# A hybrid DeltaNet and attention trunk: lower-half transfers issued one round later, scores and maxima three blocks ahead

## What is computed

```python
proj = h @ w_in + b_in                     # 16 query heads, 4 key and 4 value heads of width 64
q, k = apply_rope(q), apply_rope(k); v = ...
# chunks of 64 tokens; every chunk sees itself and the chunk before it
scores = einsum(q, k_band) * 64 ** -0.5
m = maximum(max(scores), sink)
pexp = exp(scores - m)
probs = pexp / (sum(pexp) + exp(sink - m))
o = einsum(probs, v_band)
h = h + (o @ w_out + b_out)
```

## Time and profile before

| | |
|---|---|
| median of 3 runs | 1548.16 us (1547.15 to 1553.75) |
| profiled execution | 1545.53 us, span 1543.6 us |
| mean granted TensorE clock | 0.971 of full speed |
| TensorE matmuls busy | 95% of the span |
| VectorE, ScalarE, GpSimd busy | 52%, 35%, 17% |
| keys, queries and values projected, from the first matmul to the first scores | 904.6 to 1004.6 us |
| 16 blocks, to the first output matmul | 1004.6 to 1077.0 us |

### The profile page before, as it was taken

The page is one execution under the profiler, slowest core; times in us unless marked ns, Lnnn a source line. Parts: engine busy times, 40 slices in busy tenths (PEclk is TensorE's granted clock), DMA queues, the critical chain, the costliest instruction groups (busy, mean ns, idle before and its releaser), DMA issues.

```text
span 1543.6 us, 19377 instructions
## 1 busy us (share of the span) xinstructions
PE 1467.2 (95%) x7270; PEld 1210.0 (78%) x7270; DVE 801.0 (52%) x1132; ACT 541.4 (35%) x820; POOL 262.6 (17%) x268
## 2 busy tenths in 40 slices
PE   6799999999988999999999986798999999999998
PEld 4688888888876888888888864666888888888877
DVE  4546666566657434343456664547443343434755
ACT  6333434434214314232234431145342322323444
POOL 3534435444303100000002110000201000000111
PEclk9799999999999999999999998959999999999999
DMA  5221221210112232323222326320323232323221
GB/s 144 55 55 28 55 55 27 54 37 31 41 55 95 84 109 82 109 82 108 94 98 82 94 44 140 85 60 16 109 96 109 82 110 82 109 82 109 83 82 55
DMA packets 163810, 120.73 MB, mean 78 GB/s; under 512 B 44417, under 2 KB 161442, under 8 KB 163746
## 3 DMA queue, kind: packets, MB, share of 16 engines
q1 hardware_dynamic: 152210, 116.71, 25.2%
q10 hardware_dynamic: 11536, 3.15, 0.9%
HBM read 112.50 MB, written 2.10 MB: 74 GB/s over the span
## 4 chain that ended last, share of the span: by engine, by line
PE 76%; DVE 10%; ACT 5%; issue 3%; ACTq 2%; DVEq 2%; POOL 1%; DMA 0%; POOLq 0%
PE psum L148 21%; PE psum L150 21%; PE psum L149 21%; PE psum L825 3%; PE psum L816 3%; DVE wL L140 2%; ACT wH L132 2%; PE psum L832 1%; ACTq L1693 1%; DVE bL L1269 1%; ACT taps L671 1%; DVE hT L1457 1%; PE psum L1800 1%; ACTq L1698 1%; DVE acc L1455 1%
## 5 line engine op out<-in xcount | busy, mean ns | idle before, releaser
L148 PE MATMUL psum<-aH,wH 128*128 128x512 f32 x896 | 364.2, 407 | 7.8 <-DVE wL L140 4.3
L150 PE MATMUL psum<-aL,wH 128*128 128x512 f32 x896 | 351.3, 392 | 0.0
L149 PE MATMUL psum<-aH,wL 128*128 128x512 f32 x896 | 351.1, 392 | 0.0
L140 DVE TENSOR_TENSOR wL<-wRaw,wH 128x2048 fp32r<-128x2048 f32 (+2 forms) x126 | 250.6, 1992 | 159.9 <-ACT wH L132 154.2
L148 PE MATMUL psum<-bH,wH 128*128 128x512 f32 x720 | 288.4, 401 | 25.9 <-DVE pleT L1878 19.9
L150 PE MATMUL psum<-bL,wH 128*128 128x512 f32 x720 | 283.4, 394 | 0.0
L149 PE MATMUL psum<-bH,wL 128*128 128x512 f32 x720 | 283.4, 394 | 0.0
L132 ACT CAST wH<-wRaw 128x2048 fp32r<-128x2048 f32 (+2 forms) x110 | 199.2, 1815 | 220.5 <-PE psum L150 191.8
L148 PEld LDWEIGHTS psum<-aH,wH 128*128 128x128 f32 x896 | 169.8, 189 | 41.2 <-DVE wL L140 4.7
L150 PEld LDWEIGHTS psum<-aL,wH 128*128 128x128 f32 x896 | 169.2, 189 | 36.2
L149 PEld LDWEIGHTS psum<-aH,wL 128*128 128x128 f32 x896 | 169.8, 190 | 30.7 <-issue 0.5
(11 more groups left out here) (289 smaller groups left out, 1725.8 us busy)
## 6 DMA issues: line engine op xcount, KB each, us to landing
wRaw<-in_mlp_w_up SPq DMA_DIRECT2D x64, 512.0 KB
wRaw<-in_mlp_w_down SPq DMA_DIRECT2D x64, 512.0 KB
wRaw<-in_dn_w_in SPq DMA_DIRECT2D x32, 512.0 KB
wRaw<-in_ple_w_gate SPq DMA_DIRECT2D x16, 512.0 KB
wRaw<-in_sw_w_in SPq DMA_DIRECT2D x16, 256.0 KB
wRaw<-in_sw_w_out SPq DMA_DIRECT2D x16, 256.0 KB
wRaw<-in_dn_w_out SPq DMA_DIRECT2D x8, 384.0 KB
work<-in_x SPq DMA_DIRECT2D x4, 512.0 KB, 5.1
```

The source lines that it names most:

```text
L140: last = [nc.vector.tensor_tensor(o, r, h_.bitcast(F32), ALU.subtract) for o, r, h_ in zip(*([v if half is None else v[:, half * v.shape[1 ...
L148: nc.tensor.matmul(o, wh, xh, start=first, stop=False)
L149: nc.tensor.matmul(o, wl, xh, start=False, stop=False)
L150: return nc.tensor.matmul(o, wh, xl, start=False, stop=last)
```

## The change

Two edits. In the projection, ScalarE issues the lower-half transfers of round j-1 in round j, after `prep_hi` of panel j+1 and before the copies of round j; those of the last round are issued after the loop, as before. In the blocks, scores and maxima run three blocks ahead instead of two, and `mxs` gets a third slot.

```diff
-        mxs = sqSum[:, 0:12 * GRP].rearrange("p (s a j) -> p s a j", s=2, a=6)
+        mxs = sqSum[:, 0:18 * GRP].rearrange("p (s a j) -> p s a j", s=3, a=6)
...
             scores(0)
             scores(1)
+            scores(2)
             for i in range(ATB):
-                if i + 2 < ATB:
-                    scores(i + 2)
+                if i + 3 < ATB:
+                    scores(i + 3)
...
                 prep_hi(act, n0 + j + 1, (n0 + j + 1) % 2)
                 if j == 0:
                     norm_act(act, u - 1)
+                if j:
+                    for f in range(2):
+                        stack(act, j - 1, f, 1)
                 for f in range(2):
                     act.wait_ge(qk_r, 2 * j + f + 1)
                     if j >= 4:
                         act.wait_ge(k_hi_moved[f], 16 * KVH * 2)
                     nc.scalar.copy(qkHi[j % 4][:, f, :], rot[2 * f]).then_inc(qk_hi, 1)
-                for f in range(2):
-                    stack(act, j, f, 1)
+            for f in range(2):
+                stack(act, GRP, f, 1)
...
-                t, mx = i // KVH, mxs[:, i % 2]
+                t, mx = i // KVH, mxs[:, i % 3]
...
-                t, g, mx = i // KVH, i % KVH, mxs[:, i % 2]
+                t, g, mx = i // KVH, i % KVH, mxs[:, i % 3]
...
             maxima(0)
             maxima(1)
+            maxima(2)
             for i in range(ATB):
-                mx = mxs[:, i % 2]
+                mx = mxs[:, i % 3]
...
-                if i + 2 < ATB:
+                if i + 3 < ATB:
                     dve.drain()
-                    maxima(i + 2)
+                    maxima(i + 3)
```

## The result

The changed kernel took 1531.35 us in the median of 4 runs (1527.39 to 1540.26), the kernel before 1548.76 us in 4: ratio 0.989, 95% interval 0.9841 to 0.9939. It is faster, as forecast, but by 17.4 us where 23.5 were forecast, and 1531.35 lies 0.85 us above the end of the range: the prediction was wrong. The profiled execution took 1527.39 us, span 1525.5 us, 18.1 us less than the one before.

The account below looks back on a forecast made before the run. In the projection TensorE waited on a ring through ScalarE's DMA issues. From a median of 1548.2 us, moving the transfers took off 23.5 and three ahead 0, giving 1524.7, rounded 1524.5 us; range 1511 to 1530.5.

Parts of the forecast that it names:

- the ring through ScalarE's issues: Projection: ScalarE's DMA issues delay the next cast, making rounds of 16.5 us where TensorE needs 11.2; moving them saves 23.5.
- round 2: Projection: the keys' 16 issues on ScalarE make the copies 2.8 us late, leaving TensorE one 2.8 us wait before round 3.
- a load that I had put at 6: Projection: a panel load takes 6 us; panel 3's, issued at 929.27, is due at 938.75, 9.5 us later.
- panel 4: Projection: its load lands at 945.0, 4.4 us before it is due; stretched by sharing engines, at 948, still in time.
- the clock after that wait: Projection, after the 2.8 us wait: a slower TensorE clock costs 0 or 1.6 us; 0.4 was taken.
- edit 2 cuts no link of the ring: Blocks: with scores and maxima both three ahead the order is unchanged, so two blocks at full clock still take 6.8 us.
- two blocks under 6.5 us: Blocks: sign that the prediction is wrong, meaning the ring has a link less.
- I take 0: Blocks: running three ahead gains zero, between bounds of 6.7 us won and 3.4 us lost.
- The sum: Whole kernel: 1545.5 - 23.5 = 1522.0 us for an execution like the profiled one; 1524.7 for the median, rounded 1524.5.
- a case with half clock in all blocks: Rival: the clock stays low through all blocks, ten more costing 22.6 us; 1547 us, no change; chance 0.04.
- full clock in the blocks: Rival: after the shorter wait the early blocks keep full clock, 11.3 us less, 1513 us; chance 0.22.

Follow-up runs that it names:

- edit 1 alone: Against the kernel before, only the lower-half transfers are issued one round later, scores and maxima staying two ahead; 1525.57 us, ratio 0.9854.
- edit 2 alone: Against the kernel before, only scores and maxima run three blocks ahead, transfers as before; 1551.79 us, ratio 1.0023.
- the first experiments: First follow-up kernels, sharing one chip session, edit 1 alone and edit 2 alone among them; the kernel before took 1547.38 us in 17 runs.
- The second set of the changed kernel: The changed kernel run again unaltered, against the kernel before on the same chip; median 1524.77 us of 6, ratio 0.9845.

## Why the prediction was right and where it was wrong

**Right: the ring through ScalarE's issues.** The casts follow the copies, TensorE's wait of 10.5 us is gone, those before round 4 and before the values too. From round 0's copies to the first scores it was 81.4 us before, 58.3 after; the forecast was 57.4. The change's gain up to there was shown by undoing: edit 1 alone gives the whole difference (58.3 us), edit 2 alone almost none of it (81.2).

**Right in size, half right in cause: round 2.** I let ScalarE's 16 issues begin when the cast had ended. They begin 0.25 us after it has started, beside it, and the copies came 12.25 us after round 0's in one profile and 13.41 in the other, instead of 14.2. In the second they were late by the issues, as forecast, though by about 1 us; in the first they were in time, and the landing of panel 3 stood in their place: issued at 928.41, first used at 937.18, 8.8 us for a load that I had put at 6. TensorE's wait was 2.1 us either way, not 2.8. The Trainium skill's rule in "DMA: Bandwidth & Descriptors", section "Issuing engines are not separate DMA queues", that all issuing engines share the same DMA engines, agrees with the 8.8 us: the load ran beside transfers of both queues. I weighed it for panel 4, which the cast waited 0.28 us for, and not for panel 3.

**Mis-sized, small: the clock after that wait.** I took 0.4 us between 0 and 1.6. It fell in both profiles of the changed kernel, 12.7 us for the round at 0.87, so the term was 1.6 there. Of the eleven profiles with edit 1 it fell in six, after waits of 1.81 and 2.05 to 2.14 us, and not in five, after 1.74 to 1.86. From the copies to the scores the six took 57.9 to 58.3 us, the five 56.3 to 56.5; the 57.4 of the forecast had no clock term in it. So the term is not a size between two bounds but one of two cases, and the 58.3 came near 57.4 because a wait shorter than forecast made up for part of the clock.

**Right: edit 2 cuts no link of the ring.** Two blocks took 6.77 us. That the order and not the distance closes the ring was then shown by the kernel with the maxima two ahead, 6.20 us. The prediction's sign of a ring with a link less, "two blocks under 6.5 us", is what that kernel shows.

**Wrong: "I take 0" for the blocks, and with it the top of the range.** This is the step that failed. The sum, "for an execution like the profiled one", carried over the half-clock stretch of one profile, 38 us, as if it belonged to the kernel, and gave its length no term. Measured, the stretch was 52.1 us in the profiled execution and the blocks took 5.5 us more. Its length differs between executions of one program, 41.6 and 52.1 us, and was 89.7 us for edit 1 alone. At 0.38 us for each, that is 1.3, 5.3 and 19.6 us more. I had a case with half clock in all blocks, at 22.6 us, but gave it 0.04. The kernel before has it too: 3 of its 17 runs beside the first experiments took 1564.65 to 1567.2 us, at a mean clock of 0.954, where most took 1545 to 1549 at 0.966 to 0.971. Its three runs that I had, 1547.15 to 1553.75 us, already differed by 6.6 us, and the range should have taken that in. The second set of the changed kernel, 1524.77 us, is the forecast; the first, 1531.35, is outside the range. The sum came out for executions with a short stretch, and the range had no term for the others. That the second set met the forecast within 0.3 us is luck too: it needed five short executions out of six. The opposite case, full clock in the blocks, was priced too high: of the five blocks put at 3.38 us each, the one in which the output panel is prepared took 6.6 us from transposes to transposes though nearly all of it ran at full clock (1002.70 to 1009.29 in the kernel with extra work in blocks 0 to 4), so some 8 us could have been won, by this estimate, and not 11.3.

**What stays open.** Whether three ahead lengthens the stretch somewhat: edit 2 alone lay 4.4 us above the kernel before in the median, with an interval of the ratio from 0.9984 to 1.0062. Against it, the five shorter executions of the changed kernel (up to 1525.82 us) were no longer than the four shorter ones of edit 1 alone (up to 1526.58). Why one program's executions differ at all is open, and so is why the first set of the changed kernel had lower clocks than the second. So is which property of the blocks' matmuls holds the clock down; the runs show only that it happens with TensorE busy and that, with four wide matmuls more in a block, it was short in the one profile and the clocks of all six executions were high (0.978 to 0.982).

## What to carry to other kernels

DMA issues in ScalarE's list cost it 0.7 us each here, and what counts is which instruction stands behind them: look for the place where the engine idles anyway, and give it the issues. In this ring, running further ahead helped the pace only when one side did it; where producer and consumer both moved by one, every link stayed closed. Before a clock stretch of one profile enters a sum, the spread of the runs should be asked whether it is the kernel's or the execution's, and the range should hold both.

## What the hardware showed that I had not expected

- With the wait before the scores filled, TensorE's clock fell to 0.50 and stayed there for about 75 us, although TensorE was busy in 73.1 of the 75.6 us of that stretch. In the kernel with four extra matmuls in each block it fell in the midst of work, with TensorE busy in all 4.00 us before and all 11.10 us around the fall.
- One program's half-clock stretch in the same stage differed between two executions by 10.5 us (41.6 and 52.1), and one of its six executions took 14 us longer than the longest of the others.
- DMA issues of ScalarE's list run beside its cast: the first one starts 0.25 us after the cast does.
- Fifteen issues of the same list took 10.07 us in one execution of a program and 11.23 in another.
